# Where the weight and activation buffers start in SBUF, and the reading direction of the 512-column products

## The reference

```python
x = x + gate_a * ((g_a * o_a + g_b * o_b) @ w_o)          # back to the residual, 1024 columns
h = rms_norm(x, ffn_norm) * (1.0 + scale_f) + shift_f     # block input
u = conv(h @ w_up)                                        # up-projection, 5632 columns
x = x + gate_f * ((silu(gt) * val) @ w_down)              # back to the residual, 1024 columns
```

## Time and profile before

| what | value |
|---|---|
| median of 3 runs | 1115.14 us (1115.13, 1115.14, 1118.45) |
| profiled execution, its own time | 1118.65 us |
| its span | 1117.3 us |
| mean granted TensorE clock in the span | 0.992 |
| TensorE busy, share of the span | 1091.6 us, 98% |
| VectorE / ScalarE busy | 759.7 us, 68% / 592.2 us, 53% |
| DMA queue of the loads, share of 16 engines | 51.4% |

### The profile page before, as it was taken

The page is one execution under the profiler, slowest core; times in us unless marked ns, Lnnn a source line. Parts: engine busy times, 40 slices in busy tenths (PEclk is TensorE's granted clock), DMA queues, the critical chain, the costliest instruction groups (busy, mean ns, idle before and its releaser), DMA issues.

```text
span 1117.3 us, 19183 instructions
## 1 busy us (share of the span) xinstructions
PE 1091.6 (98%) x7736; PEld 995.6 (89%) x7736; DVE 759.7 (68%) x1416; ACT 592.2 (53%) x1050; POOL 47.2 (4%) x48
## 2 busy tenths in 40 slices
PE   8999999899899999999999999999999999999998
PEld 7998888889699999789987899997889779999986
DVE  3588786997678887776677666674466466666643
ACT  4475583555576666335355744454474367444542
POOL 0260000010000000110000000000000000000000
PEclk9999998999999999999999999999999999999999
DMA  9965942554345554664442475545544134555441
GB/s 361 384 215 223 375 190 78 218 195 152 113 171 189 189 189 170 267 241 158 165 151 91 163 272 189 189 170 174 189 165 156 71 135 162 199 184 184 162 164 38
DMA packets 30764, 208.14 MB, mean 186 GB/s; under 512 B 3538, under 2 KB 4050, under 8 KB 6996
## 3 DMA queue, kind: packets, MB, share of 16 engines
q1 hardware_dynamic: 30676, 206.91, 51.4%
HBM read 205.85 MB, written 1.05 MB: 185 GB/s over the span
## 4 chain that ended last, share of the span: by engine, by line
PE 84%; DVE 11%; ACT 3%; issue 2%; DVEq 0%; ACTq 0%
PE ps L409 45%; PE ps L1730 19%; PE ps L643 3%; DVE wlo L368 3%; PE ps L1508 2%; PE ps L427 2%; DVE tm L582 2%; PE ps L2396 1%; PE ps L2428 1%; PE ps L836 1%; PE ps L1857 1%; ACT whi L360 1%; PE ps L652 1%; PE ps L1362 1%; PE ps L440 1%
## 5 line engine op out<-in xcount | busy, mean ns | idle before, releaser
L368 DVE TENSOR_TENSOR wlo<-raw,whi 128x1024 fp32r<-128x1024 f32 (+2 forms) x328 | 372.7, 1178 | 210.5 <-ACT whi L360 210.1
L360 ACT ACTIVATE whi<-raw 128x1024 fp32r<-128x1024 f32 (+2 forms) x328 | 315.7, 1011 | 156.6 <-PE ps L1730 100.8
L409 PE MATMUL ps<-H_h,whi 128*128 128x256 f32 x1376 | 390.5, 284 | 0.0
L409 PE MATMUL ps<-H_h,wlo 128*128 128x256 f32 x1376 | 385.1, 280 | 0.0
L409 PE MATMUL ps<-H_l,whi 128*128 128x256 f32 x1376 | 384.9, 280 | 0.0
L409 PEld LDWEIGHTS ps<-H_h,whi 128*128 128x128 f32 x1376 | 259.4, 189 | 1.9 <-issue 1.7
L409 PEld LDWEIGHTS ps<-H_l,whi 128*128 128x128 f32 x1376 | 259.6, 189 | 0.7 <-issue 0.5
L409 PEld LDWEIGHTS ps<-H_h,wlo 128*128 128x128 f32 x1376 | 259.9, 189 | 0.0
L1730 PE MATMUL ps<-whi,gl_h 128*128 128x512 f32 x264 | 105.3, 399 | 0.6 <-DVE wlo L368 0.6
L1730 PE MATMUL ps<-whi,gl_l 128*128 128x512 f32 x264 | 104.2, 395 | 0.0
L1730 PE MATMUL ps<-wlo,gl_h 128*128 128x512 f32 x264 | 103.8, 393 | 0.0
(11 more groups left out here) (465 smaller groups left out, 1686.7 us busy)
## 6 DMA issues: line engine op xcount, KB each, us to landing
raw<-f SPq DMA_DIRECT2D x44, 1024.0 KB, 4.8
raw<-win SPq DMA_DIRECT2D x27, 1024.0 KB, 6.8
raw<-ada SPq DMA_DIRECT2D x24, 1024.0 KB, 5.1
raw<-up SPq DMA_DIRECT2D x22, 1024.0 KB, 4.8
raw<-g SPq DMA_DIRECT2D x20, 1024.0 KB, 4.8
raw<-pw SPq DMA_DIRECT2D x12, 1024.0 KB, 4.8
raw<-down SPq DMA_DIRECT2D x10, 1024.0 KB, 5.4
raw<-wa SPq DMA_DIRECT2D x4, 1024.0 KB, 10.2
```

What stands on the lines that cost most here:

```text
L360: act.activation(whi[j % NS][:, a:b], raw_of(key)[:, a:b], ACT.Copy).then_inc(w_hi.hit(key, half), 1)
L368: dve.tensor_tensor(wlo[j % NS][:, a:b], raw_of(key)[:, a:b], whi[j % NS][:, a:b].bitcast(F32), ALU.subtract).then_inc(w_lo.hit(key, half), 1)
L409: ins_ = pe.matmul(bank[:, m * 256:(m + 1) * 256], wt[a][:, kt * w + col + m * 128:kt * w + col + m * 128 + 128], act[b][:, k0 + kt, :], s ...
```

## The change

The rule of places is rewritten: a buffer of 1024 bytes or more starts at a multiple of 128 bytes plus a `lead` given with the call, 0 if none is given. All four weight buffers start at a multiple of 128, and so does everything behind the block input (`gl`, `yc` and the rest). `H_l` starts 32 bytes and `H_h` 64 bytes past one. `par_sb` and `con_sb` are packed without rounding. In `ahead_pe` and `wide_pe` the moving operand, 512 weight columns, is read from the last column to the first, and the output is written to the PSUM bank from the last column to the first, so that each sum lands where it did. No instruction is added, removed or moved, and no wait changes.

```diff
-    place, lead = [-(-nc.sbuf_base // 64) * 64], [0]
+    place = [-(-nc.sbuf_base // 64) * 64]
-    def sb(name, shape, dt=F32):
+    def sb(name, shape, dt=F32, lead=0):
         n = 4
         for k in shape[1:]:
             n *= k
-        at = -(-(place[0] - lead[0]) // 128) * 128 + lead[0] if n >= 1024 else place[0]
+        at = place[0] if lead is None or n < 1024 else -(-(place[0] - lead) // 128) * 128 + lead
...
-    par, con = sb("par_sb", [128, NPAR]), sb("con_sb", [128, NCON])
+    par, con = sb("par_sb", [128, NPAR], lead=None), sb("con_sb", [128, NCON], lead=None)
...
-    whi, wlo = [], []
-    for i in range(NS):
-        for name, to in (("whi", whi), ("wlo", wlo)):
-            lead[0] = 32 * (len(whi) + len(wlo))
-            to.append(sb(f"{name}{i}", [128, 2048], F32R))
-    H = pair("H", 8)
+    whi = [sb(f"whi{i}", [128, 2048], F32R) for i in range(NS)]
+    wlo = [sb(f"wlo{i}", [128, 2048], F32R) for i in range(NS)]
+    H_l, H_h = sb("H_l", [128, 8, 256], F32R, 32), sb("H_h", [128, 8, 256], F32R, 64)
+    H = H_h, H_l
...
+    def back(t, a, n=256):
+
+        return t[:, a + n - 1:a - 1:-1] if a else t[:, n - 1::-1]
...
-                ins_ = pe.matmul(where[name, 0, t][:], act[h][:, ks[n], t * 128:(t + 1) * 128],
-                                 wt[a][:, kt * 512:(kt + 1) * 512], start=n == 0 and i == 0, stop=False)
+                ins_ = pe.matmul(back(where[name, 0, t], 0, 512), act[h][:, ks[n], t * 128:(t + 1) * 128],
+                                 back(wt[a], kt * 512, 512), start=n == 0 and i == 0, stop=False)
...
-                        ins_ = pe.matmul(b[t][:], act[h][:, k, t * 128:(t + 1) * 128], wt[a][:, kt * 512:(kt + 1) * 512],
+                        ins_ = pe.matmul(back(b[t], 0, 512), act[h][:, k, t * 128:(t + 1) * 128], back(wt[a], kt * 512, 512),
```

## The result

The changed kernel has a median of 1119.08 us (10 runs, 1118.08 to 1121.08) against 1115.16 (10 runs, 1114.61 to 1118.45): ratio 1.0023, 95% interval 1.0013 to 1.0033. In a second series on one chip with other kernels it was 1.0030 (1.0019 to 1.0042). By these ratios it is slower by 2.6 to 3.3 us; the two medians lie 3.9 us apart. The forecast was 7 us less. By the bound of 0.3% it is a change that can hardly be told from none; its sign is clear all the same.

The account below looks back on a forecast made before the run. TensorE's matmul pace was taken to bound the kernel. A tenth of the 71 us pool, 7 us, came off the 1115.1 us median, all other parts counting 0: 1108 us, with 8 in 10 runs from 1088 to 1132.

Parts of the forecast that it names:

- What bounds the kernel: TensorE's start-to-start matmul pace sets the time: 117.5 ns narrow (52% of the span), 232.3 ns wide (19%).
- The excess as a pool from which a place can take: fp32r matmuls at full clock take 10.8 ns (narrow) and 19.0 ns (wide) beyond one column per cycle, 71 us in all.
- two streams in each other's way: In SBUF, the moving read and the next weight load were thought to collide, making the 8 to 9% excess.
- Places count by the distance modulo 128: Matmul operands were judged by moving-to-stationary distance modulo 128 bytes; even and odd narrow units differed by 0.8 ns.
- The new set of distances does at least what the best old unit does, and a tenth of the pool besides: Narrow and wide products: 2.0 and 0.9 us gained by matching the best units; a tenth of the pool, 7 us, forecast.
- The reversed direction: Wide products read and written last to first: no row showed it; +181 us at the far end, taken as unlikely.
- Rival D: Wide products: the reversed read collides with the forward weight load, +17 us, 1132 us; chance 0.11.
- Rival E: Wide products: reversed PSUM writes run at half pace, +181 us, 1296 us; chance 0.03.
- Rival C: Narrow products: the distance 64 is a bad one, +6.4 us, 1121.5 us; chance 0.17.
- Rival B: All products: places only shuffle the meetings, pace stays within what is seen now, 1112 to 1118 us; chance 0.23.
- What the profile after would show: Narrow units alike at about 5.58 us, the 960 about 111.5 us, wide units about 5.5, L368 and L360 unchanged.
- The independent-ports rule: TensorE has two independent read ports and never waits, so no place could matter and the sum would be 0.

Follow-up runs that it names:

- f1: Whole kernel with the best placement of m5, wide products forwards: 1105.30 us against 1116.56 for the kernel before, ratio 0.9892.
- e2: The changed kernel with the wide products read and written forwards again: ratio 1.0001 to the kernel before.
- m1: Measuring kernel, matmuls alone, other engines idle, distance and direction swept: forwards at distance 0, 120.0 ns for 256 columns and 226.7 for 512.
- m5: Measuring kernel of 44 drawn buffer placements at usable addresses, forwards: the best gave 113.3 ns narrow and 231.1 wide.
- m4: Measuring kernel at the kernels' own addresses (c1's narrow ones off by 16 bytes), other engines idle, then busy: both agree to 0.01 us.
- m3: Measuring kernel with ten units in a row per setting, buffers 8320 bytes apart: narrow 119.4 ns for the places before, 118.1 changed.
- c1: Changed kernel run forwards, H_h at 16, H_l 0, gl_h and yc_h 64, gl_l and yc_l 0: ratio 1.0044 to the kernel before.
- m2: Measuring kernel in the kernel's matmul order, other engines idle, places swept, plus bf16 and a repeated column: narrow 115.6 to 120.1 ns.
- e1: The kernel before with only the wide products reversed, every buffer where it was: ratio 1.0002.
- e5: The changed kernel again, unaltered, beside the same runs of the kernel before: ratio 1.0030.

## Why the prediction was wrong

- *What bounds the kernel.* Right. In every run ahead of f1 the ratio followed from the two paces times the counts on the chain to within 1.6 us (e2 being the farthest off); the order and the engines of the chain stayed.
- *The excess as a pool from which a place can take.* Right as far as it goes: m1 and m5 show 113.3 to 120 and 226.7 to 236 by place alone, and f1 draws 12 us from it. The prediction took units "all with the same places" at 5.55 and 5.60 us as a sign of timing; m4 gives these units the same spread at fixed addresses, so the sign was weak. That one address can have two paces is shown by the changed kernel and by f1. The belief that it is two streams in each other's way is not settled: the repeated column and bf16 tie it to the reading of new columns, 32 stationary columns change it but leave most of it.
- *Places count by the distance modulo 128.* This step failed, and the forecast with it. The rows gave no ground for it beyond the alternation. The same distances modulo 128 gave, with the other engines idle, 119.4 ns in m3 and 117.5 at the kernel's own addresses in m4 (places before), and 233.6 and 240.0 (changed places, wide, reversed). c1's distances gave 115.6 in m2, 116.1 in m3 and 118.5 in the kernel. The change also put the weight buffers in another order (`whi0`, `wlo0`, `whi1`, `wlo1` became `whi0`, `whi1`, `wlo0`, `wlo1`, and `H_l` went ahead of `H_h`). By distances modulo 128 that is nothing, and the prediction does not weigh it; no run tests the order by itself.
- *The new set of distances does at least what the best old unit does, and a tenth of the pool besides.* This is the term that was wrong in sign. The narrow kind lost 0.28 ns (+1.4 us) where 0.4 and more were to be gained, and the wide kind 2.2 to 2.6 ns (+2.0 to 2.4 us) where 1.0 was to be gained: +3.4 to 3.8 us in place of -7. The tenth had no row behind it: it was taken because all distances are new, and a new placement drawn at random is more often worse than the one before than better: in m5, some 38 of 44 by the two paces and their counts. That this one lost and did not win was therefore no surprise, but the rows could not tell it.
- *The reversed direction.* Weighed as unknown, and taken as harmless in the sum. It costs 1.1 ns at the places before (e1) and about 2 (1.9 to 2.3, the changed kernel against e2) with all operands of the wide kind at 0, +1.0 to 2.1 us. Rival D had the place and the sign, and some units stand at its mark of 5.67 us and more; its price, all of the excess once more, was some eight times too high, and that the streams run towards each other was not tested. Rival E did not occur: a reversed PSUM write is free in m1. The Trainium skill, PSUM — Partial Sum Buffer, section Specifications, names patterns that are not contiguous; by these runs a descending run is not one of them.
- *Rival C*, the narrow kind a little slower, is what the places did, at a fifth of its price. Its reason, that the distance 64 is a bad one, is not borne out: in m1 it takes 117.8 ns, less than 0 and 96 (120.0 and 119.9).
- *Rival B* comes nearest with 1112 to 1118; the kernel ended a little above it, with the narrow pace inside B's bounds and the wide one outside. The independent-ports rule of the Trainium skill, SBUF — State Buffer, section Who interferes with whom, is right for the other engines, as m4 shows to 0.01 us. It does not make TensorE's pace independent of addresses.
- *What the profile after would show.* Even and odd units alike: yes, at 5.65 and not 5.58; the 960 at 113.08 and not 111.5 us; wide units at 5.60 to 5.68 and not 5.5. Durations of L368 and L360: unchanged, 372.7 and 315.6 us in all against 372.7 and 315.7.
- *Two slips in the sums*, without weight: 1118.65 less 7 is 1111.65, not 1111.5, and 3.3 / 912 is 3.6 ns, not 3.7.

Open: which addresses decide beyond the lowest seven bits, why there are several steady paces, and what picks one on entry. That entry picks it is argued from f1; no run here set the entry on purpose. It cannot be all: in the last stretch of 240 the changed kernel goes from 236.7 to 233.3 ns, and in e5 from 233.3 to 236.7, in the middle, with no gap.

## What to carry to other kernels

Where TensorE sets the time with fp32r operands, compare its start-to-start pace with half of the pace at half clock before looking elsewhere; here 8 to 9% lay there. Don't reason from distances: put the operands at the very addresses of the kernel, in its order, in a measuring kernel of nothing but matmuls; such a run told the pace of the kernel before, of e1 and of the changed kernel's narrow kind to 0.1 ns; for its wide kind it gave only one of the levels that it jumps between. Take the addresses from what the matmul reads, not from where its buffer starts. 44 placements fitted into one execution. Then build the best into the kernel and read the pace of every stage, since one placement can have two.

## What the runs showed of the hardware

- fp32r with 256 new columns takes 113.3 to 120.1 ns and with 512 takes 226.7 to 240.0 by address, order and direction, at a full clock, in rows once they have settled; 512 columns of bf16 take 215.8, one fp32r column repeated 512 times 218.7.
- The pace has steady states: the same wide code on the same addresses at 233.3, 236.7 or 240.0 ns (the changed kernel, e5, m4), steps of 3.33 ns; the same narrow unit at 113.3 or 117.8 (f1).
- A moving operand of 512 columns read from the last to the first was never faster in m1, 233.3 to 233.4 ns at every distance against 226.7 to 233.4; with 256 columns it was faster at two of four distances. A PSUM output of 512 columns written that way cost nothing.
- ScalarE, VectorE and a stream of 1 MB loads beside the matmuls changed a row of 480 by 0.01 us.
